# Twenty-one expert chunks ahead, two turns written out, and GpSimd's low parts in quarters, in a one-core two-block transformer kernel

## The reference

```python
x = x + parallel_mixer(rms_norm(x), w_in, ..., w_out)         # 8 dilated attention heads, 4 retention heads
x = x + memory_cross_attention(rms_norm(x), rms_norm(mem), ...)# 4 heads over 256 memory rows
x = x + hierarchical_moe(rms_norm(x), w_group, w_router, w1, w3, w2)
```

```python
grp  = argmax(t @ w_group)                      # one of 4 groups, its softmax value is a gate
top_vals, top_idx = top_k(e_logits[grp], 2)     # 2 of the group's 8 experts
gates = g_gate * softmax(top_vals)
y[token] += gate * (silu(xb @ w1[e]) * (xb @ w3[e])) @ w2[e]   # 32 experts, 1024 -> 512 -> 1024
```

## Time and profile before

| | |
|---|---|
| median of three runs | 1860.24 us (1855.27 to 1863.33) |
| profiled execution | 1861.57 us, of which the span of instructions is 1859.8 |
| mean granted clock of TensorE | 0.939 of full |
| busy: PE, DVE, ACT, POOL | 1660.4, 867.8, 661.6, 242.7 us |
| DMA | 421.41 MB, mean 227 GB/s |
| block 1 up to the MoE | 0 to about 272 us |
| MoE | 272 to about 742 us |
| block 2 | from there to 1860 us |

### The profile page before, as it was taken

The page is one execution under the profiler, slowest core; times in us unless marked ns, Lnnn a source line. Parts: engine busy times, 40 slices in busy tenths (PEclk is TensorE's granted clock), DMA queues, the critical chain, the costliest instruction groups (busy, mean ns, idle before and its releaser), DMA issues.

```text
span 1859.8 us, 29654 instructions
## 1 busy us (share of the span) xinstructions
PE 1660.4 (89%) x11817; PEld 1325.8 (71%) x11817; DVE 867.8 (47%) x1292; ACT 661.6 (36%) x965; POOL 242.7 (13%) x182
## 2 busy tenths in 40 slices
PE   8989997677667776999999999999999999899997
PEld 6777874343223332899977779998999977779996
DVE  4684542011101111555565656555655575665555
ACT  5454441111101111343433544444334333544442
POOL 1223210000000000000133323001300133232000
PEclk9999998887788888999999999999999999899999
DMA  9514476999999999945533055436454542054511
GB/s 387 181 47 142 176 271 262 426 425 426 426 426 426 426 426 402 357 170 186 198 138 134 1 182 204 178 120 247 170 197 175 198 152 103 7 211 179 191 45 45
DMA packets 60951, 421.41 MB, mean 227 GB/s; under 512 B 7008, under 2 KB 16064, under 8 KB 17216
## 3 DMA queue, kind: packets, MB, share of 16 engines
q1 hardware_dynamic: 59136, 409.13, 56.1%
q10 hardware_dynamic: 1728, 11.03, 1.7%
HBM read 419.08 MB, written 1.05 MB: 226 GB/s over the span
## 4 chain that ended last, share of the span: by engine, by line
PE 62%; SPq 13%; DMA 8%; DVE 5%; issue 4%; ACT 3%; POOL 3%; DVEq 0%; ACTq 0%; POOLq 0%
PE bank L964 26%; SPq L1618 13%; PE bank L1005 12%; DMA ring<-in_we 7%; PE bank L1697 6%; PE bank L1739 6%; PE bank L1765 2%; DMA ring<-in_wf 1%; PE bank L1882 1%; PE bank L1900 1%; PE bank L983 1%; POOL small L534 1%; PE bank L604 1%; PE bank L1877 1%; PE bank L990 1%
## 5 line engine op out<-in xcount | busy, mean ns | idle before, releaser
L964 PE MATMUL bank<-xh,wlu 128*128 128x256 f32 x1344 | 379.9, 283 | 0.0
L964 PE MATMUL bank<-xh,whu 128*128 128x256 f32 x1344 | 379.8, 283 | 0.0
L964 PE MATMUL bank<-xl,whu 128*128 128x256 f32 x1344 | 379.8, 283 | 0.0
L964 PEld LDWEIGHTS bank<-xh,whu 128*128 128x128 f32 x1344 | 257.0, 191 | 3.3
L964 PEld LDWEIGHTS bank<-xl,whu 128*128 128x128 f32 x1344 | 257.0, 191 | 3.3
L964 PEld LDWEIGHTS bank<-xh,wlu 128*128 128x128 f32 x1344 | 257.2, 191 | 0.0
L873 DVE TENSOR_TENSOR wlu<-ring,whu 128x2048 fp32r<-128x2048 f32 x84 | 196.1, 2334 | 50.9 <-ACT whu L868 50.9
L873 DVE TENSOR_TENSOR wld<-ring,whd 128x1024 fp32r<-128x1024 f32 x88 | 108.2, 1229 | 189.2 <-ACT whd L868 189.2
L868 ACT ACTIVATE whu<-ring 128x2048 fp32r (+1 forms) x88 | 167.1, 1901 | 3.0 <-DMA ring<-in_wf 3.0
L868 ACT ACTIVATE whd<-ring 128x1024 fp32r (+1 forms) x88 | 93.2, 1060 | 207.1 <-PE bank L1005 203.7
L604 PE MATMUL bank<-ring,xg 128*32 128x256 f32 x1472 | 110.4, 436 | 48.7 <-DMA ring<-in_we 46.3
(11 more groups left out here) (319 smaller groups left out, 2808.3 us busy)
## 6 DMA issues: line engine op xcount, KB each, us to landing
ring<-in_we SPq DMA_DIRECT2D x144, 1024.0 KB, 26.9
ring<-in_wf SPq DMA_DIRECT2D x88, 1536.0 KB, 6.6
ring<-in_w SPq DMA_DIRECT2D x52, 1024.0 KB, 4.8
more<-in_we SPq DMA_DIRECT2D x48, 1024.0 KB, 25.7
ring<-in_w SPq DMA_DIRECT2D x32, 256.0 KB, 3.6
ln<-in_ln ACTq DMA_DIRECT2D x6, 1024.0 KB, 4.8
bias<-in_bias ACTq DMA_DIRECT2D x2, 2048.0 KB, 7.8
bias<-in_bias SPq DMA_DIRECT2D x1, 2048.0 KB, 19.7
```

Of the source, the lines that this page charges most:

```text
L964: ins = pe.matmul(bank[4 + p][:, m * S:(m + 1) * S], w[p][:, cols], v[:, k], start=(k == 0 and n == 0), stop=(k == KD - 1 and n == 2))
```

## The change

It has five parts.

1. Five more places for expert chunks (EXTRA = 5), used once each, in buffers that are free by then: two behind the key and query transposes of the memory attention, two in the work area, one in the transposed input of the logits. SyncE issues 21 chunks before the first refill, in a written order of places, each with its own wait. The next 27 are issued straight, outside any loop, and only then is the number of turns read.
2. Turns 0 and 1 are written out on PE, ACT and DVE; the registers are loaded behind them. The zero matmuls move ahead of the routing, and `pe_keep` of 15 and of 5 stands ahead of the rank matmuls and behind them. The first turn's one-hot is made ahead of the turn count. The gather reads raw `x` with a one-hot scaled by rs (`ohr`, two more DVE instructions a turn); the copy `xn` (two ACT instructions) is gone. The first two expert chunks wait for the first half of `xg` only, and the transposes of `ohg` stand behind them.
3. Low parts on POOL, and the cast of L1555, are four instructions of 512 columns instead of one of 2048.
4. The queries of units without bias are scaled when their transposes are copied out of PSUM; L1969 is gone, and the exponential has the scale 1.
5. In-projection of block 2: ACT's high part of chunk 1 no longer waits for the FFN's end, its low part moves from DVE to POOL, ahead of the powers; `top` and `rest` of the norm run in pairs; TensorE starts chunk 0 with the two products that need xh alone.

```diff
-            last_pair = load_pairs(pe)
-            pe.wait_ge(gcol_ok, 1)
-            pe.wait_ge(xn_ok, 1)
             for b in range(4):
                 ins = pe.matmul(bank[b][:], zeros[:, 0:P], zeros[:], start=True, stop=False, skip_group_check=True)
             ins.then_inc(m_sc, 1)
+            pe_keep(pe, 5, 15)
+
+            pe.wait_ge(r_ok, 2)
+            pe.matmul(bank[RANK][:, 0:NE], before[:], chosen[:, 0], start=True, stop=True)
...
+            pe_keep(pe, 5, 5)
+            pe.wait_ge(gcol_ok, 1)
...
+                            ins = pe.matmul(bank[4 + half][:, k * P:(k + 1) * P],
+                                            x[:, i, (4 * half + k) * P:(4 * half + k + 1) * P],
+                                            ohr[:, i].rearrange("p e s -> p (e s)"), start=(i == 0), stop=(i == 1))
...
+                            if e == 0 and c == 2:
+                                weights_T(it)
+                            if e == 0 and c % 2 == 0:
+                                pe.wait_ge(m_xg, it * 2 + (c // 2 + 1))
...
+            for t in range(2):
+                turn(None, t)
+            last_pair = load_pairs(pe)
+            with pe.Fori(0, last_pair) as prev:
+                for t in range(2):
+                    turn(prev, t)
```

```diff
+            rows_of(0, 0, 0)
+            st.link(dve.tensor_reduce(gs[:, 46:47], bank[RANK][:, 2 * NE:3 * NE], X, ALU.max))
...
+                for i in range(NT):
+                    dve.wait_ge(dve_loop, it * 2 + (i + 1))
+                    ins = dve.tensor_scalar(ohr[:, i], oh[:, i], rs[:, i:i + 1], None, ALU.mult)
+                ins.then_inc(m_oh, 1)
```

```diff
+            for free in (12, 13, 0, 1, 2, 3, 10, 11, 14, 15, 4, 16, 17, 5, 6, 8, 7, 9, 18, 19, 20):
...
+                elif free < ESLOTS + 2:
+                    sp.wait_ge(t_ps, 34)
+                elif free == ESLOTS + 2:
+                    sp.wait_ge(d_used, DENSE1)
+                elif free == ESLOTS + 3:
+                    sp.wait_ge(sumsq, 4)
                 else:
-                    sp.wait_ge(o_ok, UNITS1)
-                expert_chunk(0, j)
+                    sp.wait_ge(r_ps, 1)
+                expert_chunk(0, by_slot[free], by_slot[free])
+            used = 2 * TURN
+            for j in range(ESLOTS + EXTRA, used):
+                sp.wait_ge(e_used, j - ESLOTS - EXTRA + 1 if j < 2 * ESLOTS + EXTRA else j - ESLOTS + 1)
+                expert_chunk(0, j, j)
             last_pair = load_pairs(sp)
```

```diff
+            for c0 in range(0, CH, step):
+                part = slice(c0, c0 + step)
+                ins = eng.tensor_tensor(slot_r[n % SLOTS1][:, part], slot[n % SLOTS1][:, part],
+                                        high1[n % 2][:, part].bitcast(F32), ALU.subtract)
+            ins.then_inc(low_at(n)[0], 1)
```

```diff
             if unit.bias is None:
-                st.link(dve.tensor_reduce(nmax[:, b], src, X, ALU.max, negate=True))
-                dve.tensor_scalar(nmax[:, b], nmax[:, b], unit.scale, None, ALU.mult).then_inc(lg_ok, 1)
+                dve.tensor_reduce(nmax[:, b], src, X, ALU.max, negate=True).then_inc(lg_ok, 1)
                 return
...
-                act.wait_ge(f_dn, (l * 2 + 1) * (FT + 1))
                 act_high(act, run, 1)
...
-                low(pool, run2(l, 0), 0)
+                for c in range(2):
+                    low(pool, run2(l, 0), c, 512)
```

```diff
+                if split:
+                    for passes in ((0, 1), (2,)):
+                        if passes == (2,):
+                            pe.wait_ge(t_out, tb + 1)
+                        for kk in range(per):
+                            for i in range(NT):
+                                ins = products(kk, i, halves, passes)
```

More of the change, by code:

```diff
@@ L121, in build @@
         iota = sb("iota", [P, S])
+        rel_at = here[0]
         rel = sb("rel", [P, 2, NT, S])
@@ new lines, in turn @@
+                pe.wait_ge(m_yA, it * 4 + TEAM)
+                pe.wait_ge(m_yV, it * 4 + TEAM)
+                for i in range(NT):
+                    for c in range(2):
+                        ins = pe.matmul(bank[2 * i + c][:], sT[:, tok(i)], yg[:, c * 512:(c + 1) * 512],
+                                        start=False, stop=False, skip_group_check=True)
+                        ins.then_inc(m_bk if i + c < 2 else m_sc, 1)
+            for t in range(2):
+                turn(None, t)
@@ L696, in act_moe @@
                 out(it, 3)
+            turn(0)
+            turn(1)
+            last = load_turns(act)
+            with act.Fori(2, last + 1) as it:
+                turn(it)
             act_first(act, 0)
@@ L795, in dve_moe @@
                 out(it, 3)
+            turn(0)
+            rows_of(1, 1, 0)
+            turn(1)
+            last = load_turns(dve)
+            with dve.Fori(2, last + 1) as it:
+                rows_of(it, it % TEAMS, it // TEAMS)
+                turn(it)
             dve_first(dve, 0)
@@ L1172, in rest @@
                 dve.tensor_tensor(pair(xl, q), pair(xf, q), pair(high, q).bitcast(F32), ALU.subtract).then_inc(t_out, 1)
-            if then is None:
+            if paired:
+                for q in range(4):
+                    top(q)
+                    rest(q)
+            else:
                 for q in range(4):
@@ L1178, in dve_norm_T @@
                     rest(q)
-            else:
-                for q in range(4):
-                    top(q)
-                    rest(q)
-                    if q == 0:
-                        then()
         def last_norm(dve, st, j, scale, waits):
@@ L1554, in pool_layers @@
                 pool.sem_inc(hi_go, 1)
-                pool.tensor_copy(run.highs[0], slot[run.slots[0]]).then_inc(dh_ok, 1)
+                for c0 in range(0, CH, 512):
+                    ins = pool.tensor_copy(run.highs[0][:, c0:c0 + 512], slot[run.slots[0]][:, c0:c0 + 512])
+                ins.then_inc(dh_ok, 1)
                 for c in range(2):
-                    low(pool, run, c)
+                    low(pool, run, c, 512)
                 g = l * 2 + 1
@@ L1681, in pe_part @@
             for c in range(first, end):
-                if tb is not None:
+                split = tops is not None and c == first
+                if split:
+                    pe.wait_ge(xh_ok, tops)
+                elif tb is not None:
                     pe.wait_ge(t_out, tb + (c - first + 1))
```

294 lines of the change are left out of this document (143 added, 151 removed).

## The result

The changed kernel takes 1831.18 us, the median of four runs (1827.54 to 1832.79); the kernel before, timed beside it, 1860.60 (1855.27 to 1863.33). The ratio is 0.9837, with a 95% interval of 0.9816 to 0.9858: 29.4 us less. The profiled execution has a span of 1829.1 us against 1859.8. The forecast was 1830.6, range 1821 to 1844.

A forecast was written before the change was run, and what follows sets the result against it. Transfers at 426 GB/s bound the MoE, TensorE's gaps and clock the rest. Terms -17.4 (MoE), -0.6, +1.1, -0.5, -12.2 sum to -29.6 against 1861.6: 1832.0, or 1830.6 on the median; range 1821 to 1844.

The forecast's parts named there:

- First expert chunk earlier: MoE entry, routing to gather: first refill at 290.0 instead of 295.10, -5.1 us; bounds about -2.5 (clock falls anyway) and -6.
- half clock in 278 to 290: Sign at the MoE's entry: TensorE at half clock there, or a refill at 293, would refute the earlier start.
- Five chunks: MoE: five more chunks issued ahead travel in the idle stretch, 5 x 2.461 = -12.3 us.
- Quarters: GpSimd low parts cut in four: +0.37 us per chunk, fewer VectorE waits; block 1 -0.6, three norms +1.1.
- my third rival: VectorE low parts slip between quarters and hold up six GpSimd chunks, up to 2.3 us each: 1842.2 us; chance 0.07.
- In-projection: Norm and start of block 2's in-projection: -0.25 us net per layer, -0.5 in both; bounds -1.5 and +2.5.
- Tail of the mixer: Last eight attention units: out-projection at 1070.4 instead of 1076.06; with scalings -6.1 us per layer, -12.2 in both.
- clock at 1.00 to the out-projection: Sign in the mixer's tail: full clock from 1060 to the out-projection; about 3.9 of each 6.1 us is the clock.
- The slower one: Straight code of written-out turns waits behind weight chunks, 26.6 us per packet; five give 1924 us; chance 0.04.
- a clock that falls in the tail anyway: Short idles remain in the mixer's tail, so 2 x 3.9 us comes back: 1838.4 us; chance 0.16.
- The MoE that gains only its start: Chunks ahead not done in the idle stretch, or first refills wait for something else: 1842.9 us; chance 0.07.
- a change that does less than it says: Later refills still wait for the turn count, block 2's gains lost too: within 0.5%; chance 0.04.

The follow-up runs named there:

- whole lows: Changed kernel with every GpSimd low part and the cast in one 2048-column instruction again, scaled queries kept: 1832.28 us.
- in-projection as before: Changed kernel with the in-projection part undone, except the pairs of `top` and `rest`: 1830.75 us.
- both undone: Changed kernel with whole low parts and the scaling of the maximum put back together, MoE as changed: 1840.18 us.
- three with keeping matmuls in the tail: Changed kernel with keeping matmuls added in the mixer's tail: alone 1826.75 us; also at the MoE's entry 1823.62; those plus later in-projection scales 1816.98.
- fewer quarters: Changed kernel with keeping matmuls added at entry and tail, and GpSimd quarters only where a small VectorE operation lay beside: 1828.87 us.
- keeping matmuls in the tail alone: Changed kernel with 3 keeping matmuls ahead of each of a layer's last two units' values and 3 behind the last, none added in the MoE: 1826.75 us.
- sixteen chunks: Changed kernel with 16 expert chunks ahead instead of 21 (EXTRA = 0, other order of places), all else kept: 1841.62 us.
- the square: In to out, us: neither quarters nor scaled queries 129.4 and 127.6; queries alone 124.7 (layer 1); quarters alone 122.6 twice; both 123.2 twice.
- one moved call: Kernel with keeping matmuls added at entry and tail, in-projection scales on VectorE moved behind chunk 7's low part: 1816.98 us.

## Why the prediction was right, point by point

**The sum.** -29.6 was forecast against the profiled execution and -30.7 came; on the medians 29.4 came. The direction, the size and the order of the terms held. Part of the closeness is luck. The start gave 2.8 us less than forecast; 1.1 us more in the MoE and 2.5 us that nobody forecast made up for it. And in the tail two errors cancelled, as shown below.

**First expert chunk earlier.** This is the term that was mis-sized: -5.1 forecast, -2.26 in the profile. The first refill came at 291.97 and not at 290, and by the prediction's own sign (half clock in 278 to 290) the start was refuted in part. The steps themselves were right where the clock was up: in six profiles in which the clock was up at the logits and up again by the ranks and the gather (whole lows, in-projection as before, both undone, and three with keeping matmuls in the tail) first logit matmul to first refill is 16.9 to 17.1 us, 5.6 less than before the change. In a seventh, with fewer quarters, the seventeen keeping matmuls ran partly at half clock and ended late, and it is 17.54. The kernel with keeping matmuls in the tail alone shows where its 5.5 us lie: the ranks end 0.9 earlier behind the first logit, from there to the gather it takes 1.56 us instead of 4.11 (turn count, zero matmuls and register loads are out of the way), the gather is 0.9 shorter, the first expert chunk starts 0.9 sooner behind it and gives its place back 0.3 sooner. No run puts the loop or the copy `xn` back alone. I had put the fall of the clock into the bounds (-2.5) as something behind the logits. In the first profile it came inside them, and cost twice: 2.2 us in the logits and 1.3 us in which fifteen keeping matmuls at double price stood in the ranks' way. The lower bound (-2.5) named just this, and -2.26 lies a little beyond it.

**Five chunks.** 12.3 forecast; 12.13 between the two kernels that differ in it (and in the order of the places) alone. The piece in the changed kernel lost 13.44. The kernel with sixteen chunks is already 1.31 below the kernel before (439.78 against 441.09), so this part does not come from chunks ahead; what it is was not taken apart. In other profiles of the same MoE the piece is 425.8 instead of 427.6, but the piece behind it is then 202.5 instead of 200.7, so the end of the FFN gains nothing.

**Quarters.** 5.0 us for four (4.97 to 5.05 in most places) against 4.54 to 4.61 for one: +0.4, forecast +0.37. The start-up of 0.13 us per piece stood in no row ahead of the runs; they give about 0.14. The norms paid 0.97 instead of 1.1. In block 1 the stall of 4.52 us is a chain of short ones:

```profile
91.13 1.24 DVE L2488 TENSOR_SCALAR small<-small 128x8 f32<-128x8 f32 x1 [0.69 <-ACT small L2337]
92.65 0.93 DVE L2490 TENSOR_SCALAR small<-small 128x8 f32<-128x8 f32 x1 [0.28 <-ACT small L2339]
93.61 1.20 DVE L2491 TENSOR_TENSOR small<-small 128x8 f32<-128x8 f32 x1
94.85 1.22 DVE L2492 TENSOR_SCALAR small<-small 128x8 f32<-128x8 f32 x1
```

In these rows of the changed kernel each of four small operations waits for a quarter of its own, 0.9 to 1.2 us, where rows 6 have one wait for the whole. About 1.4 us of the gain reached TensorE, and other chunks gave most of it back. Apart from the kernel with fewer quarters (267.12), the first logit matmul comes anywhere from 270.1 to 272.5, because the clock falls in one to three places of block 1, not the same in every profile, and one such fall moves it by about 1.5 us. The kernel with both undone has its falls where the changed kernel has them (20, 92 and 170 us), and there it is 272.07 with whole low parts against 271.59 with quarters: 0.5 us, forecast 0.6. The kernel with fewer quarters did better still, by about 1.5. That VectorE holds up a quarter in turn, my third rival, is seen in one place: a chunk at 127.06 took 6.02 us instead of 5.0, one of its quarters 2.26 us beside an operation of VectorE of 1.48 us. It didn't matter for the time. Both kinds of wait agree with what the Trainium skill says under "SBUF — State Buffer", "Who interferes with whom": the wait is for one whole instruction, whichever came first.

**In-projection.** -0.25 forecast per layer, -0.35 measured, and undoing it cost 0.34 and 0.38. The power stood behind GpSimd's second low part at 922.39, 2.0 us behind the end of the FFN where it was 1.1, as the steps had it.

**Tail of the mixer.** -6.1 forecast per layer, -6.11 and -5.76 measured in the piece. But the step "clock at 1.00 to the out-projection" failed in both layers: the fall came at the last unit. In layer 1 it took 1.2 us (123.18 against 122.0 with the clock held in the tail), in layer 0, where it lasted twice as long, 2.8 (123.24 against 120.43 with no fall in the layer). In layer 0 a fall at the end of the in-projection, which the kernel before had and the changed one had not, hid 1.6 of that. With the clock held as forecast the term would have been -6.9 to -7.3 and not -6.1: it was too small by about 1 us, and the clock took that away again. And I gave both edits the credit together, where the square shows that either would have done; the -0.4 for the scalings themselves came as 0.5.

**What nobody forecast.** 1.36 us behind the MoE, of which 0.57 lie in FFN 1 of layer 0 (188.47 against 187.90), at whose start the clock of the kernel before was down (747.4 to 750.8), and 1.16 us at the start of FFN 1 of layer 1, where it was down as well (0.60 over 4 us) and that of the changed one up. In the kernels whose second tile is quartered the FFNs took 187.9 to 188.0, 189.1, 189.1 and 189.1 us in every profile; with whole tiles two kernels of three had one or both of the last two at 190.3 to 190.5 (the kernel before and the one with whole low parts; not the one with both undone). Why was not tried.

**Rivals.** The slower one, code of the written-out turns waiting behind weights, did not come: TensorE's longest wait of kind "issue" in the expert matmuls is 1.6 us, and 64 instruction packets moved in place of 66. Whether a packet waits long when an engine needs it can't be read from these runs, since none did. The rival of a clock that falls in the tail anyway was half true. The MoE that gains only its start is out by the sixteen chunks. The one of quarters held up by VectorE came in one place, and the one of a change that does less than it says not at all.

## What to carry to other kernels

Where a transfer-bound stage follows a stretch without transfers, each transfer moved into that stretch is worth its full length (2.43 us here for 1 MB), for as long as there is idle time to fill. A small operation held up by a long one on another engine can be cured on either side, by removing it or by cutting the long one. Look which is cheaper: here the removal saved 0.5 us more, and each cut cost 0.4 us where GpSimd was on the path. Short idles of TensorE ahead of a dense stage are worth filling, and behind such an idle it pays to look at what its releaser itself waited for: one moved call was worth 6.6 us here (1823.62 to 1816.98, and in the profiles 2.5 us in layer 0 and 4.1 in layer 1), where cutting the in-projection's low parts brought 0.35 per layer.

## What the runs showed of the hardware that I had not expected

- Idles of 0.78 us, twice within 3 us, stand ahead of a fall to half clock in the last unit of a layer; with three keeping matmuls in each of them, and three behind, the clock held in eight tails of eight, without them in four of sixteen.
- The same code has its clock fall at different places in different executions (logits at 5.96 or 3.73 us), and one fall lasted 17 us at half clock with TensorE busy throughout, costing 8 us. The runs of one kernel lie 5 to 16 us apart, so one or two such falls would fill that distance.
- A subtraction of 512 columns on GpSimd takes 1.29 us in the median, of 2048 columns 4.59, and four in a row 5.0: cutting in four costs 0.4 us, not more.
